# Compressed-branch logits with the keys stationary in four column groups, turned back for a four-head-wide softmax, in a one-core hybrid decoder block

## The chip, the cores and the metric

One core of one Trainium2 chip runs the program. The metric is the device time of one execution in microseconds; a kernel's time is the median over its runs. Every tensor is float32. The large products are made of three passes on split operands (a high part and the remainder, in a 32-bit format that TensorE reads in one pass).

## The reference, cut to what matters

The block is a token mixer of two branches (a gated delta rule and a native sparse attention) and a SwiGLU behind it, for 256 tokens and 1024 channels. The change sits in the compressed branch of the sparse attention: 8 heads in 2 groups, 15 compressed keys and values per group, two tiles of 128 tokens.

```python
kc = rmsnorm(compress(kc_raw, cmp_pe[0], cmp_w1[0], cmp_w2[0]), k_norm_w[0])   # (B, 15, G, 128)
vc = compress(vc_raw, cmp_pe[1], cmp_w1[1], cmp_w2[1])
lc = einsum("bqgrd,bngd->bgrqn", qb, kc) * scale + head_bias(t[:, None] - cmp_end[None, :])
pc = masked_softmax(lc, cmp_end[None, :] <= t[:, None])
oc = einsum("bgrqn,bngd->bqgrd", pc, vc)
o = gb[..., 0:1] * oc + gb[..., 1:2] * o_s + gb[..., 2:3] * ow
```

With 256 tokens the selected-block branch takes every block, so the other two branches are two causal attentions over 256 keys.

## The kernel before, in words

The program is written engine by engine, with semaphores by hand; nothing schedules it. All weights come as 87 chunks of 1 MB (`CHUNKS`), in order, through three buffers `raw`. For most chunks ACT makes `w_hi` (L502) and DVE `w_lo` (L791), two buffers of each, and PE runs 24 matmuls per half of a chunk (L1201 to L1203). The chunks of the compression MLP (`cmpk`, `cmpv`, four each) aren't split: PE runs four matmuls per half on four column groups, with 32 columns stationary and 256 moving (L1273).

Between the halves of the chunks, in slots (n, half), stand pieces of other work. Every engine walks through the same slots, and within a slot in the order: half chunk, stages of the delta rule, `misc`, attention `unit`.

- Stages of the delta rule (`gdn`): each goes over four groups of problems b = 0 to 3, in a ring of three PSUM banks, so that group 3 waits until the bank of group 0 has been read. In slots (24,0) to (27,1) they are X4, Y4, T4, X5, Y5, T5, X6, Z6; an X (L1367) or T (transposes of `Db`, L1206) is read by ACT (L643), a Y (L1333) by DVE (L929), Z6 is L1378. In (28,0), (28,1), (29,0) and (29,1) follow w0, s1, v1 and o1.
- `misc(m)`: the steps of the attention around one PSUM bank `log_ps`, each of which waits on PE for the output of the one before it (`m_out`). Before, in this order: W2_K and TURN_KC (compressed keys, turned into `kcT`), TURN_KS (24,1), TURN_KW (25,0), LOGITS_C (25,1), TURN_PC to TURN_PC+3 in (28,0), (28,1), (29,0), (29,1), and W2_V (30,0).
- LOGITS_C before: 16 matmuls on PE (L1433), one per head and token tile, with 128 columns of `nqT` stationary and 15 columns of `kcT` moving. Each is two records in the trace. DVE then masks, scales by the query norm, adds the bias and subtracts the maximum (L1028 to L1036), ACT takes the exponential (L681), DVE sums, divides and applies the gate (L1039 to L1045). On DVE all that stands in (25,1), ahead of the reading of Y5.
- TURN_PC before: 16 transposes in four slots of four (L1206), each read by ACT into `pcT` (L685) on 15 partitions.
- W2_V: four matmuls (L1423) and ACT's copy to `vc` (L678) on 15 partitions.
- Units: from (31,0) on, one per half chunk, over 8 heads by 2 token tiles. PE makes logits (L1449) once DVE has read those of the unit before (L1058, L1059), and adds the compressed branch's share by L1471.

In (29,1) ACT squares the delta rule's output (L662, 16 instructions), then does the rest of its slot, evacuates chunk 29 and makes `w_hi` of chunk 31; DVE makes `w_lo` of chunk 31 from that, and PE needs it for (31,0).

Of the kernel before, what the change touches and what calls it, by code (L numbers as in the profile page):

```python
# [119 lines left out]
def slot_solves(n, half):  # L120
# [5 lines left out]

W2_K, TURN_KC, TURN_KS, TURN_KW, LOGITS_C, TURN_PC, W2_V = 0, 1, 2, 3, 4, 5, 9
MISC_SLOTS = {W2_K: (AT["kw", 0], 0), TURN_KC: (AT["cmpv", 0], 0), TURN_KS: (AT["cmpv", 0], 1), TURN_KW: (AT["cmpv", 1], 0),
              LOGITS_C: (AT["cmpv", 1], 1),
              TURN_PC: (AT["vs", 0], 0), TURN_PC + 1: (AT["vs", 0], 1), TURN_PC + 2: (AT["vw", 0], 0), TURN_PC + 3: (AT["vw", 0], 1),  # L130
              W2_V: (AT["gz", 0], 0)}

# [11 lines left out]
def hybrid_block(nc, x, norm1_w, w_in, conv_w, a_log, dt_bias, gdn_norm_w, cmp_pe, cmp_w1, cmp_w2,  # L144
# [5 lines left out]
    with ctx:  # L150
# [329 lines left out]
        def _(act):  # L480
# [184 lines left out]
            def misc(m):  # L665
                if m in (TURN_KS, TURN_KW):
                    act.wait_ge(m_pe, m + 1)
                    j = 0 if m == TURN_KS else 1
                    dst = (ksT, kwT)[j][:].rearrange("p g (t c) -> p t g c", t=TT)
                    nc.scalar.activation(dst, log_ps[:].rearrange("p (t g c) -> p t g c", t=TT, g=GROUPS), ACT.Copy,  # L670
                                         scale=wk[:, 1 + j:2 + j]).then_inc(m_out, 1)
                elif m == TURN_KC:
                    act.wait_ge(m_pe, m + 1)
                    nc.scalar.activation(kcT[:, :, 0:NCMP], log_ps[:, 0:32].rearrange("p (g c) -> p g c", g=GROUPS)[:, :, 0:NCMP],
                                         ACT.Copy, scale=wk[:, 0:1]).then_inc(m_out, 1)
                elif m == W2_V:
# [99 lines left out]
        def _(dve):  # L776
# [238 lines left out]
            def misc(m):  # L1015
                if m == W2_K:
# [7 lines left out]
                    nc.vector.tensor_tensor(kc[:], kc[:], scol["d"][0:NCMP, 4:6].unsqueeze(2).to_broadcast([NCMP, GROUPS, DH]), ALU.mult).then_inc(m_out, 1)  # L1024
                elif m == LOGITS_C:
                    dve.wait_ge(m_pe, m + 1)
                    lg = log_ps[:, 0:HEADS * TT * 16].rearrange("p (h t n) -> p h t n", h=HEADS, t=TT)
                    link(nc.vector.memset(pc[:], NEG))  # L1028
                    for t in range(TT):
                        k = NCMP if t else (P - CMP_BLOCK) // CMP_STRIDE + 1  # L1030
                        first = P * (1 - t) + CMP_BLOCK - 1
# [10 lines left out]
                    link(nc.vector.tensor_scalar(pcs[:, :, 0], pcs[:, :, 0], rowvalid[:], None, ALU.mult))
                    g0 = gates[:].rearrange("p t (h b) -> p h t b", b=3)[:, :, :, 0]
                    link(nc.vector.tensor_tensor(pcs[:], pcs[:], g0, ALU.mult))
                    nc.vector.tensor_tensor(pc[:].rearrange("p h t n -> p (h t) n"), pc[:].rearrange("p h t n -> p (h t) n"),  # L1045
                                            pcs[:].rearrange("p h t -> p (h t)").unsqueeze(2).to_broadcast([P, 16, NCMP]), ALU.mult).then_inc(m_out, 1)

# [149 lines left out]
        def _(pe):  # L1197
# [209 lines left out]
            def misc(m):  # L1407

                if m >= 1:
                    pe.wait_ge(m_out, m)  # L1410
                if m in (TURN_KS, TURN_KW):
                    j = 0 if m == TURN_KS else 1
                    pe.wait_ge(key_n, j + 1)
                    for q in range(4):
                        last = transpose(log_ps[:, q * P:(q + 1) * P], key_tok[:, j, q, :])
                elif m in (W2_K, W2_V):
                    c = 0 if m == W2_K else 1
                    pe.wait_ge(hid_done, c + 1)
                    if c == 0:
                        pe.wait_ge(rk_ready, 1)  # L1420
                    for g in range(GROUPS):
                        for a in range(2):
                            last = pe.matmul(log_ps[0:NCMP, g * DH:(g + 1) * DH], hid[:, c, a, g * 16:g * 16 + NCMP], cmp2[:, c, a, :],  # L1423
                                             start=(a == 0), stop=(a == 1))
                elif m == TURN_KC:
                    for g in range(GROUPS):
                        last = transpose(log_ps[:, g * 16:g * 16 + NCMP], kc[:, g, :], NCMP)
                elif m == LOGITS_C:
                    pe.wait_ge(copied, COPY_NO[AT["nq", 3]] + 1)
                    for h in range(HEADS):  # L1430
                        for t in range(TT):
                            o = (h * TT + t) * 16
                            last = pe.matmul(log_ps[:, o:o + NCMP], nqT[:, h, t * P:(t + 1) * P], kcT[:, h // 4, 0:NCMP], start=True, stop=True)  # L1433
                else:
                    for q in range(4):
                        h, t = UNITS[4 * (m - TURN_PC) + q]
                        last = transpose(log_ps[0:NCMP, q * P:(q + 1) * P], pc[:, h, t, :])
                last.then_inc(m_pe, 1)

            def unit(i):  # L1440
                if i < len(UNITS):
                    h, t = UNITS[i]
                    w = P * (t + 1)
                    if i >= 1:
                        pe.wait_ge(s_done, i)
                    else:
                        pe.wait_ge(m_out, 10)
                    for a, keys in enumerate((ksT, kwT)):
# [114 lines left out]
```

## Time and profile before

| | |
|---|---|
| median of 3 runs | 647.7 us (646.86 to 649.11) |
| the profiled execution's own time | 654.54 us |
| its span, first to last instruction | 652.2 us |
| PE / DVE / ACT / POOL busy | 94% / 59% / 48% / 6% of the span |
| chain that ended last, by engine | PE 82%, DVE 10%, ACT 5%, issue 2%, DMA 1% |
| mean granted TensorE clock | 0.973 |
| DMA | 97.98 MB, 150 GB/s over the span |

"Idle before" in a row is the time its engine stood still ahead of it, with the one that ended it. "issue" names no other engine. PEclk in a table of windows is the TensorE clock that was granted, as a share of 2.4 GHz: 0.50 is 1.2 GHz. PE rows overlap, since matmuls are pipelined; the distance between the starts of two groups is what the first one takes.

### The profile page before, as it was taken

Reading aid. Unit: us, or ns where it says so; the run is one execution under the profiler, and the core shown is the slowest. Engines: PE = TensorE matmul, PEld = TensorE weight load, DVE = VectorE, ACT = ScalarE, POOL = GpSimd, SP = SyncE. Lnnn points to the kernel's source line nnn. Section 1 sums busy time; section 2 is a strip of 40 time slices with the busy share of each in tenths; the row PEclk is TensorE's granted clock in tenths of the full one; section 3 lists DMA queues with packets and bytes.
Section 4 is the critical chain, followed back from the end, with each engine's and each line's share of the span. In section 5 each row is a group of like instructions: output and inputs, shape, how many; then the busy total and the mean of one; then the engine's idle time right before and its main releaser. Section 6 shows DMA issues by size and latency. Waiting matters only on the chain.

```text
span 652.2 us, 10734 instructions
## 1 busy us (share of the span) xinstructions
PE 610.6 (94%) x4344; PEld 560.3 (86%) x4344; DVE 382.2 (59%) x651; ACT 311.7 (48%) x526; POOL 35.9 (6%) x55
## 2 busy tenths in 40 slices
PE   3998999998899999789899999997999999999996
PEld 2988999897798899789799999996888888888885
DVE  5566778773573534567746465555565566665553
ACT  5458864433325335554454454433655544444441
POOL 4100000330510000010000000000000000000000
PEclk9999999998989899989989999999799999999999
DMA  8942545165554262323333355547166666666631
GB/s 266 294 152 71 186 132 162 34 205 178 171 142 130 65 194 66 118 76 96 100 112 118 100 189 190 183 146 193 64 186 182 191 182 187 183 189 190 194 125 65
DMA packets 110458, 97.98 MB, mean 150 GB/s; under 512 B 4690, under 2 KB 106127, under 8 KB 110410
## 3 DMA queue, kind: packets, MB, share of 16 engines
q1 hardware_dynamic: 108272, 93.69, 47.2%
q0 software_dynamic: 1632, 2.47, 1.6%
q10 hardware_dynamic: 506, 1.14, 0.5%
q8 instruction: 35, 0.57, 0.4%
q14 instruction: 13, 0.11, 0.0%
HBM read 96.52 MB, written 1.45 MB: 150 GB/s over the span
## 4 chain that ended last, share of the span: by engine, by line
PE 82%; DVE 10%; ACT 5%; issue 2%; DMA 1%; DVEq 0%; ACTq 0%
PE ps L1201 15%; PE ps L1202 15%; PE ps L1203 15%; PE ps L1292 13%; PE ps L1295 6%; PE ps L1206 4%; PE ps L1333 4%; ACT w_hi L502 3%; DVE w_lo L791 3%; PE ps L1474 2%; PE ps L1367 2%; PE ps L1449 2%; PE ps L1273 1%; DVE cacc L884 1%; PE ps L1471 1%
## 5 line engine op out<-in xcount | busy, mean ns | idle before, releaser
L791 DVE TENSOR_TENSOR w_lo<-raw,w_hi 128x2048 fp32r<-128x2048 f32 x78 | 178.6, 2292 | 150.2 <-ACT w_hi L502 150.2
L502 ACT ACTIVATE w_hi<-raw 128x2048 fp32r<-128x2048 f32 x78 | 148.8, 1910 | 77.3 <-PE ps L1203 74.0
L1201 PE MATMUL ps<-h_both,w_hi 128*128 128x256 f32 x480 | 141.2, 294 | 5.4 <-ACT w_hi L502 3.0
L1202 PE MATMUL ps<-h_both,w_hi 128*128 128x256 f32 x480 | 137.9, 287 | 0.0
L1203 PE MATMUL ps<-h_both,w_lo 128*128 128x256 f32 x480 | 137.7, 287 | 0.0
L1292 PE MATMUL ps<-h_both,w_hi 128*128 128x512 f32 x352 | 122.9, 399 | 0.9 <-issue 0.9
L1201 PEld LDWEIGHTS ps<-h_both,w_hi 128*128 128x128 f32 x480 | 94.2, 196 | 7.6 <-issue 4.4
L1202 PEld LDWEIGHTS ps<-h_both,w_hi 128*128 128x128 f32 x480 | 94.3, 196 | 0.3 <-issue 0.2
L1203 PEld LDWEIGHTS ps<-h_both,w_lo 128*128 128x128 f32 x480 | 94.1, 196 | 0.0
L1295 PE MATMUL ps<-h_both,w_lo 128*128 128x256 f32 x352 | 91.5, 280 | 0.0
L1292 PEld LDWEIGHTS ps<-h_both,w_hi 128*128 128x128 f32 x352 | 64.2, 189 | 13.5 <-issue 1.1
L1295 PEld LDWEIGHTS ps<-h_both,w_lo 128*128 128x128 f32 x352 | 67.0, 190 | 3.8
L698 ACT ACTIVATE sc<-sc,s_nm 128x128 f32<-128x128 f32 (+1 forms) x32 | 14.3, 448 | 49.5 <-DVE s_nm L1059 49.5
L1201 PE MATMUL ps<-w_hi,g_hi 128*128 128x512 f32 x88 | 34.3, 389 | 0.0
L1202 PE MATMUL ps<-w_lo,g_hi 128*128 128x512 f32 x88 | 34.2, 389 | 0.0
L1203 PE MATMUL ps<-w_hi,g_lo 128*128 128x512 f32 x88 | 34.2, 389 | 0.0
L550 ACT ACTIVATE usum<-ps 128x256 f32<-128x256 f32 x22 | 8.4, 383 | 51.4 <-PE ps L1292 51.4
L884 DVE SCALAR_TENSOR_TENSOR cacc<-cin,cols_a,cacc 128x256 f32<-128x256 f32 x72 | 29.5, 478 | 0.0
L1201 PE MATMUL ps<-w_hi,h_both 128*128 128x256 f32 x64 | 19.8, 309 | 3.0 <-ACT w_hi L502 3.0
L1078 DVE TENSOR_TENSOR usum<-usum,ps 128x256 f32<-128x256 f32 x22 | 9.2, 420 | 18.3 <-ACT usum L550 18.3
L1202 PEld LDWEIGHTS ps<-w_lo,g_hi 128*128 128x128 f32 x88 | 16.5, 188 | 3.5
L1203 PEld LDWEIGHTS ps<-w_hi,g_lo 128*128 128x128 f32 x88 | 16.5, 188 | 3.5
(341 smaller groups left out, 1070.2 us busy)
## 6 DMA issues: line engine op xcount, KB each, us to landing
raw<-in_w_in SPq DMA_DIRECT2D x34, 1024.0 KB, 5.2
raw<-in_w_gate SPq DMA_DIRECT2D x22, 512.0 KB, 4.0
raw<-in_w_up SPq DMA_DIRECT2D x22, 512.0 KB, 5.3
raw<-in_w_down SPq DMA_DIRECT2D x11, 1024.0 KB, 4.9
raw<-in_cmp_w SPq DMA_DIRECT2D x8, 1024.0 KB, 6.1
raw<-in_w_proj_a SPq DMA_DIRECT2D x4, 1024.0 KB, 5.0
raw<-in_w_proj_b SPq DMA_DIRECT2D x4, 1024.0 KB, 5.1
raw<-in_w_out SPq DMA_DIRECT2D x4, 1024.0 KB, 5.1
```

What stands on the lines that cost most here:

```text
L502: nc.scalar.activation(w_hi[s % NSPL][:], raw[n % NRAW][:], ACT.Copy).then_inc(hi_done, 1)
L698: nc.scalar.activation(sc[i % 3][:, a, 0:w], sc[i % 3][:, a, 0:w], ACT.Exp, bias=scol["nm"][:, 2 * (i % 3) + a:2 * (i % 3) + a + 1], accum ...
L791: nc.vector.tensor_tensor(w_lo[s % NSPL][:], raw[n % NRAW][:], w_hi[s % NSPL][:].bitcast(f32), ALU.subtract).then_inc(lo_done, 1)
L884: ins = nc.vector.scalar_tensor_tensor(acc, src[:, a, j:j + SEQ], tap(k, a, j), acc, ALU.mult, ALU.add)
L1201: pe.matmul(bank, lhs(lh), rhs(rh), start=start, stop=False)
L1202: pe.matmul(bank, lhs(lh), rhs(rl), start=False, stop=False)
L1203: return pe.matmul(bank, lhs(ll), rhs(rh), start=False, stop=stop)
L1206: return pe.transpose(o, i, ident[0:n, 0:n])
L1292: cross = lambda stop: pe.matmul(bank[:], hi[:, k, half * P:(half + 1) * P], h_both[:, :, k, :], start=(k == 0), stop=stop)
L1295: last = pe.matmul(bank[:, 0:SEQ], lo[:, k, half * P:(half + 1) * P], h_hi[:, k, :], start=False, stop=False)
L1333: mm = lambda q, lhsT, rhs, start=True, stop=True: pe.matmul(b4[:, q, :], lhsT, rhs, start=start, stop=stop)
L1367: last = pe.matmul(b4[:, q, c], p4(ATb)[:, q, :], p4(Db)[:, q, c], start=True, stop=True)
```

## The change

- LOGITS_C moves to (25,0), ahead of TURN_KW. It is now four matmuls: 32 columns of `kcT` (15 keys, padded by zeros) stationary in column group c, the 512 columns of heads 2c and 2c+1 moving. The result has (column group, key) on the partitions. ACT copies it to `sc[0]` (512 columns).
- TURN_LC is new, in (26,0): four 128x128 transposes turn it back to tokens on the partitions, and DVE and ACT do the softmax, for each of the four blocks (head parity a, token tile t) four heads wide, with rows of 32 of which 15 count. On DVE it now stands behind the reading of Y5.
- TURN_PC is one step of four 128x128 transposes in (28,1), read by one ACT copy. (28,0), (29,0) and (29,1) have none.
- TURN_KW moves from (25,0) to (25,1). W2_V makes its product four times over, on four partition groups: eight matmuls with 16 columns stationary. In the units L1471 reads rows 32(h//2) and on.
- POOL clears `kcT` at the start.

```diff
+W2_K, TURN_KC, TURN_KS, LOGITS_C, TURN_KW, TURN_LC, TURN_PC, W2_V = range(8)
+MISC_SLOTS = {W2_K: (AT["kw", 0], 0), TURN_KC: (AT["cmpv", 0], 0), TURN_KS: (AT["cmpv", 0], 1), LOGITS_C: (AT["cmpv", 1], 0),
+              TURN_KW: (AT["cmpv", 1], 1), TURN_LC: (AT["cmpv", 2], 0), TURN_PC: (AT["vs", 0], 1), W2_V: (AT["gz", 0], 0)}
...
+            nc.gpsimd.memset(kcT[:], 0.0).then_inc(ones_set, 1)
...
                 elif m == LOGITS_C:
+                    act.wait_ge(m_pe, m + 1)
+                    nc.scalar.activation(sc[0][:].rearrange("p a c -> p (a c)"), log_ps[:], ACT.Copy).then_inc(m_out, 1)
+                elif m == TURN_LC:
                     act.wait_ge(pc_s, 1)
                     nc.scalar.activation(pc[:], pc[:], ACT.Exp).then_inc(pc_e, 1)
-                elif m >= TURN_PC:
+                elif m == TURN_PC:
                     act.wait_ge(m_pe, m + 1)
-                    q = 4 * (m - TURN_PC)
-                    nc.scalar.activation(pcT[:, q:q + 4, :], log_ps[0:NCMP, :].rearrange("p (a c) -> p a c", a=4), ACT.Copy).then_inc(m_out, 1)
+                    nc.scalar.activation(pcT[:], log_ps[:].rearrange("p (a c) -> p a c", a=2 * TT), ACT.Copy).then_inc(m_out, 1)
...
-                elif m == LOGITS_C:
+                elif m == TURN_LC:
                     dve.wait_ge(m_pe, m + 1)
...
                     link(nc.vector.memset(pc[:], NEG))
-                    for t in range(TT):
+                    for b in range(2 * TT):
+                        a, t = b // TT, b % TT
                         k = NCMP if t else (P - CMP_BLOCK) // CMP_STRIDE + 1
                         first = P * (1 - t) + CMP_BLOCK - 1
...
+                        link(nc.vector.tensor_tensor(pc[:, b, :, 0:k], lg[:, b, :, 0:k], of_head(col["rn"], a, t).unsqueeze(2).to_broadcast([P, 4, k]), ALU.mult))
+                        link(nc.vector.tensor_tensor(pc[:, b, :, 0:k], pc[:, b, :, 0:k],
+                                                     bias_g[:, a:HEADS:2, first:first + CMP_STRIDE * (k - 1) + 1:CMP_STRIDE], ALU.add))
+                    link(nc.vector.tensor_reduce(pcm[:], valid, AX.X, ALU.max))
+                    nc.vector.tensor_tensor(valid, valid, pcm[:].unsqueeze(3).to_broadcast([P, 2 * TT, 4, NCMP]), ALU.subtract).then_inc(pc_s, 1)
                     dve.wait_ge(pc_e, 1)
...
+                elif m == W2_V:
+                    pe.wait_ge(hid_done, 2)
+                    for a in range(2):
+                        for c in range(4):
+                            g = c // 2
+                            last = pe.matmul(log_ps[32 * c:32 * c + 16, 0:DH], hid[:, 1, a, g * 16:(g + 1) * 16], cmp2[:, 1, a, :],
                                              start=(a == 0), stop=(a == 1))
...
-                    for h in range(HEADS):
-                        for t in range(TT):
-                            o = (h * TT + t) * 16
-                            last = pe.matmul(log_ps[:, o:o + NCMP], nqT[:, h, t * P:(t + 1) * P], kcT[:, h // 4, 0:NCMP], start=True, stop=True)
...
+                    for c in range(4):
+                        last = pe.matmul(log_ps[32 * c:32 * c + 32, :], kcT[:, c // 2, :], nqT[:, 2 * c:2 * c + 2, :].rearrange("p h c -> p (h c)"),
+                                         start=True, stop=True)
+                elif m in (TURN_LC, TURN_PC):
+                    for b in range(2 * TT):
+                        src = sc[0][:].rearrange("p a c -> p (a c)")[:, b * P:(b + 1) * P] if m == TURN_LC else pc[:, b].rearrange("p c n -> p (c n)")
+                        last = transpose(log_ps[:, b * P:(b + 1) * P], src)
...
-                        pe.wait_ge(m_out, 10)
+                        pe.wait_ge(m_out, W2_V + 1)
...
+                    rows = slice(32 * (h // 2), 32 * (h // 2) + kk)
+                    pe.matmul(o, vc[rows, :], pcT[rows, (h % 2) * TT + t, :], start=True, stop=False)
```

The order of PE before, slots (25,0) to (27,0), from T4 (`ps<-ident,Db`) to X6 (`128x64`):

```order
L1206 MATMUL ps<-ident,Db 128x128 x16
L1206 MATMUL ps<-ident,key_tok 128x128 x4
L1273 MATMUL ps<-raw_50,flat 32x256 x4
L1367 MATMUL ps<-Db,ATb 128x128 x16
L1433 MATMUL ps<-kcT,nqT 128x15 x16
L1273 MATMUL ps<-raw_51,flat 32x256 x4
L1333 MATMUL ps<-AXb,DTb 128x128 x16
L1273 MATMUL ps<-raw_51,flat 32x256 x4
L1206 MATMUL ps<-ident,Db 128x128 x16
L1273 MATMUL ps<-raw_49,flat 32x256 x4
L1367 MATMUL ps<-Db,ATb 128x64 x16
```

The same stretch of PE in the changed kernel:

```order
L1212 MATMUL ps<-ident,Db 128x128 x16
L1442 MATMUL ps<-nqT,kcT 32x512 x4
L1279 MATMUL ps<-raw_50,flat 32x256 x4
L1373 MATMUL ps<-Db,ATb 128x128 x16
L1212 MATMUL ps<-ident,key_tok 128x128 x4
L1279 MATMUL ps<-raw_51,flat 32x256 x4
L1339 MATMUL ps<-AXb,DTb 128x128 x16
L1212 MATMUL ps<-ident,sc_122 128x128 x4
L1279 MATMUL ps<-raw_51,flat 32x256 x4
L1212 MATMUL ps<-ident,Db 128x128 x16
L1279 MATMUL ps<-raw_49,flat 32x256 x4
L1373 MATMUL ps<-Db,ATb 128x64 x16
```

The logits now stand right ahead of a half chunk, TURN_KW (`key_tok`) behind X5, and four transposes of `sc` (TURN_LC) between Y5 and T5.

On ACT, before, the reading of X5 (`AXb`), the exponential (`pc<-pc`) and the reading of T5 (`DTb`):

```order
L670 ACTIVATE kwT<-ps,wk 128x2x2x128
L643 ACTIVATE AXb<-ps 128x512 x4
L681 ACTIVATE pc<-pc 128x240
L643 ACTIVATE DTb<-ps 128x512 x4
L502 ACTIVATE w_hi_52<-raw_50 128x2048
```

And now:

```order
L681 ACTIVATE sc_122<-ps 128x512
L642 ACTIVATE AXb<-ps 128x512 x4
L669 ACTIVATE kwT<-ps,wk 128x2x2x128
L684 ACTIVATE pc<-pc 128x512
L642 ACTIVATE DTb<-ps 128x512 x4
L501 ACTIVATE w_hi_52<-raw_50 128x2048
```

The exponential keeps its place ahead of the reading of T5. On DVE the instructions that it waits for moved from ahead of the reading of Y5 to behind it:

```order
L992 TENSOR_TENSOR key_tok<-key_tok,s_c 128x512
L931 COPY_PREDICATED Db<-levels,ps 128x512 x8
L1032 MEMSET pc 128x512
L1037 TENSOR_TENSOR pc<-ps,c_rn 128x4x7
L1038 TENSOR_TENSOR pc<-pc,bias_g 128x4x7
```

Before, four of the eight (Y5's) stood behind the last instruction of the softmax.

## Rows read from the trace of the kernel before

**Rows 1.** Waits of PE, 264 to 375 us: total, times, longest

```profile
PE ps L1449 <- DVE s_nm L1059: 5.0, 3, 2.1
PE ps L1423 <- ACT pcT L685: 1.6, 1, 1.6
```

**Rows 2.** Timeline, PE, 205 to 224 us: start, us, instruction

```profile
205.82 0.60 PE L1206 MATMUL ps<-ident,key_tok 128*128 128x128 f32 x4
...
206.35 0.64 PE L1273 MATMUL ps<-raw,flat 128*32 128x256 f32 x8
...
206.92 3.84 PE L1367 MATMUL ps<-Db,ATb 128*128 128x128 f32 x32
...
210.60 3.64 PE L1433 MATMUL ps<-kcT,nqT 128*128 128x15 f32 x32
...
214.17 1.06 PE L1273 MATMUL ps<-raw,flat 128*32 128x256 f32 x8
...
215.16 4.12 PE L1333 MATMUL ps<-AXb,DTb 128*128 128x128 f32 x24
...
221.19 2.00 PE L1206 MATMUL ps<-ident,Db 128*128 128x128 f32 x16
...
223.69 3.79 PE L1367 MATMUL ps<-Db,ATb 128*128 128x64 f32 x32
```

**Rows 3.** Tile pc: duration ns min/median/max, first and last start us

```profile
L1032 DVE TENSOR_TENSOR pc<-ps,c_rn x2: 217/249/281, 214.7 to 215.2; 128x56 f32<-128x56 f32 x1, 128x120 f32<-128x120 f32 x1
L1033 DVE TENSOR_TENSOR pc<-pc,bias_g x2: 256/307/358, 214.9 to 215.5; 128x56 f32<-128x56 f32 x1, 128x120 f32<-128x120 f32 x1
L1028 DVE MEMSET pc<- x1: 258/258/258, 214.4 to 214.4; 128x240 f32 x1
L1035 DVE TENSOR_REDUCE pcm<-pc x1: 402/402/402, 215.9 to 215.9; 128x16 f32<-128x240 f32 x1
L1036 DVE TENSOR_TENSOR pc<-pc,pcm x1: 408/408/408, 216.3 to 216.3; 128x240 f32<-128x240 f32 x1
L681 ACT ACTIVATE pc<-pc x1: 403/403/403, 216.8 to 216.8; 128x240 f32<-128x240 f32 x1
```

**Rows 4.** Timeline: Y4 on PE, its last reading on DVE, T4's on ACT

```profile
199.22 3.84 PE L1333 MATMUL ps<-AXb,DTb 128*128 128x128 f32 x32
...
203.09 0.73 DVE L929 COPY_PREDICATED Db<-levels,ps 128x512 f32<-128x512 uint8 x1 [0.16 <-PE ps L1333]
...
204.68 2.07 ACT L643 ACTIVATE DTb<-ps 128x512 f32<-128x512 f32 x4 [0.47 <-PE ps L1206]
```

**Rows 5.** Windows: us, busy of PE, PEld, DVE, ACT, POOL; PEclk, DMA share, GB/s

```profile
262.70:264.30 1.60, 0.01 (x1) 0.02 (x2) 0.00 (x0) 1.60 (x10) 0.00 (x0) 1.00 0.00 0
264.30:268.40 4.10, 4.09 (x32) 3.60 (x32) 1.78 (x1) 2.47 (x3) 0.00 (x0) 1.00 0.00 0
284.00:285.90 1.90, 0.08 (x2) 0.04 (x1) 1.84 (x4) 0.06 (x1) 0.00 (x0) 1.00 0.00 0
285.90:289.40 3.50, 3.50 (x10) 2.47 (x10) 2.21 (x6) 1.09 (x5) 0.00 (x0) 0.51 0.88 293
320.50:322.60 2.10, 0.00 (x0) 0.00 (x0) 2.07 (x6) 0.00 (x0) 0.00 (x0) 1.00 1.00 283
322.60:330.30 7.70, 7.66 (x32) 6.55 (x33) 3.69 (x11) 5.33 (x14) 0.00 (x0) 0.56 0.17 58
...
214.26:217.60 3.34, 3.34 (x19) 2.53 (x20) 2.56 (x8) 0.40 (x1) 0.00 (x0) 0.50 0.00 0
```

**Rows 6.** The chain that ended last: the first of the four TURN_PC

```profile
238.70 0.44 PE ps L1206 x4
```

**Rows 7.** Timeline, 266 to 277 us, DVE and PE

```profile
266.62 2.29 DVE L791 TENSOR_TENSOR w_lo<-raw,w_hi 128x2048 fp32r<-128x2048 f32 x1 [5.30 <-ACT w_hi L502]
269.01 0.36 PE L1201 MATMUL ps<-h_both,w_hi 128*128 128x256 f32 x1 [0.62 <-issue]
276.51 0.70 PE L1449 MATMUL ps<-ksT,nqT 128*128 128x256 f32 x2 [1.07 <-DVE s_nm L1059]
```

More of the change, by code:

```diff
@@ L121, in slot_solves @@
     return 2 * (n - FIRST_STAGE_SLOT) + half - 1 == BEFORE_SOLVE + SOLVE_AFTER
[L127 to L131, printed above, removed]
+W2_K, TURN_KC, TURN_KS, LOGITS_C, TURN_KW, TURN_LC, TURN_PC, W2_V = range(8)
+MISC_SLOTS = {W2_K: (AT["kw", 0], 0), TURN_KC: (AT["cmpv", 0], 0), TURN_KS: (AT["cmpv", 0], 1), LOGITS_C: (AT["cmpv", 1], 0),
+              TURN_KW: (AT["cmpv", 1], 1), TURN_LC: (AT["cmpv", 2], 0), TURN_PC: (AT["vs", 0], 1), W2_V: (AT["gz", 0], 0)}
 def slot_misc(n, half):
@@ L180, in hybrid_block @@
         key_tok = at("key_tok", yb_at + 12 * KB, [P, 2, 4, DH])
-        pcT = at("pcT", yb_at, [NCMP, 16, P])
+        pcT = at("pcT", yb_at + 9 * KB, [P, 2 * TT, P])
+        pcm = at("pcm", yb_at + 11 * KB, [P, 2 * TT, 4])
+        pcs = at("pcs", yb_at + 11 * KB + 64, [P, 2 * TT, 4])
         arena = take(72 * KB)
@@ L265, in hybrid_block @@
         xs = own("xs", [P, TT, 4])
-        kcT = own("kcT", [P, GROUPS, 16])
+        kcT = own("kcT", [P, GROUPS, 32])
         ps = [ctx.enter_context(nc.psum_tensor(f"ps{i}", [P, 512], f32)) for i in range(8)]
@@ L1024, in misc @@
                     nc.vector.tensor_tensor(kc[:], kc[:], scol["d"][0:NCMP, 4:6].unsqueeze(2).to_broadcast([NCMP, GROUPS, DH]), ALU.mult).then_inc(m_out, 1)
-                elif m == LOGITS_C:
+                elif m == TURN_LC:
                     dve.wait_ge(m_pe, m + 1)
-                    lg = log_ps[:, 0:HEADS * TT * 16].rearrange("p (h t n) -> p h t n", h=HEADS, t=TT)
+                    lg = log_ps[:].rearrange("p (b c n) -> p b c n", b=2 * TT, c=4)
+                    of_head = lambda hts, a, t: hts[:, :, t].rearrange("p (c a) -> p a c", a=2)[:, a, :]
+                    valid = pc[:, :, :, 0:NCMP]
@@ L1038, in misc @@
+                        link(nc.vector.tensor_tensor(pc[:, b, :, 0:k], pc[:, b, :, 0:k],
+                                                     bias_g[:, a:HEADS:2, first:first + CMP_STRIDE * (k - 1) + 1:CMP_STRIDE], ALU.add))
+                    link(nc.vector.tensor_reduce(pcm[:], valid, AX.X, ALU.max))
+                    nc.vector.tensor_tensor(valid, valid, pcm[:].unsqueeze(3).to_broadcast([P, 2 * TT, 4, NCMP]), ALU.subtract).then_inc(pc_s, 1)
                     dve.wait_ge(pc_e, 1)
-                    link(nc.vector.tensor_reduce(pcs[:].rearrange("p h t -> p (h t)"), pc[:].rearrange("p h t n -> p (h t) n"), AX.X, ALU.add))
+                    link(nc.vector.tensor_reduce(pcs[:], valid, AX.X, ALU.add))
@@ L1040, in misc @@
                     link(nc.vector.reciprocal(pcs[:], pcs[:]))
[L1042 to L1046, printed above, removed]
+                    by_t = pcs[:].rearrange("p (a t) c -> p t a c", t=TT)
@@ new lines, in misc @@
+                    link(nc.vector.tensor_scalar(by_t[:, 0], by_t[:, 0], rowvalid[:], None, ALU.mult))
+                    g0 = gates[:].rearrange("p t (c a b) -> p t a c b", a=2, b=3)
+                    for t in range(TT):
+                        ins = nc.vector.tensor_tensor(by_t[:, t], by_t[:, t], g0[:, t, :, :, 0], ALU.mult)
+                    link(ins)
+                    nc.vector.tensor_tensor(valid, valid, pcs[:].unsqueeze(3).to_broadcast([P, 2 * TT, 4, NCMP]), ALU.mult).then_inc(m_out, 1)
@@ L1415, in misc @@
                         last = transpose(log_ps[:, q * P:(q + 1) * P], key_tok[:, j, q, :])
[L1416 to L1420, printed above, removed]
+                elif m == W2_K:
+                    pe.wait_ge(hid_done, 1)
+                    pe.wait_ge(rk_ready, 1)
                     for g in range(GROUPS):
                         for a in range(2):
-                            last = pe.matmul(log_ps[0:NCMP, g * DH:(g + 1) * DH], hid[:, c, a, g * 16:g * 16 + NCMP], cmp2[:, c, a, :],
+                            last = pe.matmul(log_ps[0:NCMP, g * DH:(g + 1) * DH], hid[:, 0, a, g * 16:g * 16 + NCMP], cmp2[:, 0, a, :],
+                                             start=(a == 0), stop=(a == 1))
+                elif m == W2_V:
[4 more added lines that the diff above has]
+                            last = pe.matmul(log_ps[32 * c:32 * c + 16, 0:DH], hid[:, 1, a, g * 16:(g + 1) * 16], cmp2[:, 1, a, :],
                                              start=(a == 0), stop=(a == 1))
@@ L1429, in misc @@
                     pe.wait_ge(copied, COPY_NO[AT["nq", 3]] + 1)
-                    for h in range(HEADS):
-                        for t in range(TT):
-                            o = (h * TT + t) * 16
-                            last = pe.matmul(log_ps[:, o:o + NCMP], nqT[:, h, t * P:(t + 1) * P], kcT[:, h // 4, 0:NCMP], start=True, stop=True)
[L1434 to L1437, printed above, removed]
+                    for c in range(4):
[5 more added lines that the diff above has]
+                        last = transpose(log_ps[:, b * P:(b + 1) * P], src)
                 last.then_inc(m_pe, 1)
@@ L1470, in unit @@
                     kk = NCMP if t else (P - CMP_BLOCK) // CMP_STRIDE + 1
-                    pe.matmul(o, vc[0:kk, g, :], pcT[0:kk, j, :], start=True, stop=False)
+                    rows = slice(32 * (h // 2), 32 * (h // 2) + kk)
+                    pe.matmul(o, vc[rows, :], pcT[rows, (h % 2) * TT + t, :], start=True, stop=False)
                     for a, values in enumerate((vs, vw)):
```

15 lines of the change are left out of this document (4 added, 11 removed).

## The prediction

> **What bounds the kernel now.** The chain that ended last is PE for 82% of the span, so I read PE's waits first and the timeline of the slots that change next. Between 205 and 262 us PE hardly waits for another engine. Behind that, up to 375 us, stand two waits that matter here: 1.6 us for ACT's last `pcT` copy, and three waits of units for DVE, 5.0 us in all [rows 1]. So until 262 us what PE issues is the time, and the logits alone, 16 matmuls of 15 moving columns, take from 210.60 to 214.17: 3.57 us [rows 2]. A second cost stands right behind them. From 214.26 to 217.6 PE is granted 1.2 GHz instead of 2.4 [rows 5], though it was never idle before: what it ran was the 15-column matmuls. The half chunk at 214.17 takes 0.99 us instead of 0.57 (206.35 to 206.92), and three quarters of Y5 behind it 4.12 us [rows 2], where all of Y4 takes 3.84 us [rows 4].
>
> All sums go by the profiled execution (span 652.2 us, own time 654.54 us, 1.1% above the median 647.7 us). I apply the differences to the median unscaled. About 0.3% (2 us) is what a measurement of this kernel can tell from no change.
>
> **Term A, slots (25,0) to X6.** I count from 205.82, where T4 ends in both. Before, X6 starts at 223.69: 17.87 us [rows 2]. The changed order on PE, if it never waits:
> - four logits matmuls with 512 columns. The four of a half chunk, also on four column groups but with 256 columns, take 0.57 us up to the next work, of which I put 0.15 down to the change of work. Twice the columns: 2 x 0.42 + 0.15 = 1.0. Bounds: 0.57 below; above 3.6, if the groups don't overlap (Y4's 32 records of 128 columns start 0.112 apart [rows 4], so eight of 512 would take 8 x 0.45; for 256 columns the same sum gives 1.8, and the row shows 0.57). I take 1.0, since the nearest row overlaps.
> - half chunk 0.57, X5 3.68 (206.92 to 210.60), TURN_KW 0.53, half chunk 0.57, Y5 3.68 at full clock: so Y5 starts at 205.82 + 1.0 + 0.57 + 3.68 + 0.53 + 0.57 = 212.17.
> - TURN_LC 0.53 (as TURN_KW), half chunk 0.57, T5 and a half chunk 2.50 (221.19 to 223.69).
> Together 1.0 + 0.57 + 3.68 + 0.53 + 0.57 + 3.68 + 0.53 + 0.57 + 2.50 = 13.63: X6 at 219.45, 4.24 us earlier.
>
> But there is a new wait. ACT now reaches the reading of T5 only behind the exponential, and the exponential waits for DVE, which starts on the logits only behind Y5. DVE ends its last copy of Y4 at 203.82, 4.60 us after Y4's start [rows 4]; the same behind Y5 gives 216.77. Then, from the durations of [rows 3] with 0.04 us between linked instructions (2.18 us of work lie between 214.4 and 216.8):
> - memset of 512 instead of 240 columns: 0.258 + 272 x 1.05 ns = 0.54;
> - two pairs on 28 elements and two on 60, read off the line through 56 and 120: multiply 0.19 and 0.22, add 0.21 and 0.26, so 2 x 0.40 + 2 x 0.48 = 1.76;
> - maximum 0.40, subtraction 0.41; ten gaps 0.4.
> That is 3.51 us: 220.28. The exponential of 512 columns takes 0.6 (0.40 for 240, and ACT's copies of 512 take some 0.6), the reading of T5's first group another 0.6 [rows 4]: 221.45. PE has made three groups of T5 by 216.95 + 3 x 0.45 = 218.30 and then stands still, since the ring has three banks, for **3.15 us**. X6 starts at 222.6, 1.1 us earlier than before instead of 4.24. If the new DVE instructions cost nothing beyond their old 2.4 us the wait is 2.1; if each strided one costs 0.1 more it is 4.
>
> A rule speaks against the change here. The Trainium skill, TensorEngine Tiling (Array Packing), section Performance Considerations, says that tiling speeds up TensorE but not the evacuation of PSUM, so that the copy may become the bottleneck. By PE's own rows alone the term would be 4.24 us; by that rule it's the 1.1.
>
> **The clock behind that wait.** The trace has stretches in which PE was idle and what followed: after 1.9 us at 284 it was granted 1.2 GHz for 3.4 us, after 2.1 us at 320.5 for most of 7.7 us (0.56 on average), after 1.6 us at 262.7 it kept 2.4 GHz [rows 5]. A wait of 3.15 us is longer than all of these, so I expect a stretch at 1.2 GHz. Part of it falls into the wait, and X6 has only 64 columns per pass, so that the weights set its pace: I take 1.3 us, between 0.4 (most of it hidden) and 3.4 (a long one as at 322.6). The old stretch behind the 15-column logits is in the 17.87 us, so it's already counted as gone. Term A: 1.1 - 1.3 = **-0.2 us**.
>
> **Term B, TURN_PC.** Four steps become one. Two of the removed ones, in (28,0) and (29,0), stand ahead of o1 on a PE that doesn't wait: 2 x 0.44 [rows 6] = **0.9 us**. The one kept has 128 instead of 15 partitions, and the transposes have the same 128 columns: nothing. ACT's copy is of 512 columns as before.
>
> **Term C, from o1 to unit 1.** The third removed step was the one PE waited for 1.6 us [rows 1]. That wait goes, but not into the time: chunk 31 can't start before its `w_lo`, which ends at 268.91, and PE starts at 269.01 [rows 7]. `w_lo` hangs on `w_hi`, and this on ACT's queue behind the 16 squares; what leaves this queue is one `pcT` copy, 0.5 us. So PE's two waits, 1.6 and 0.6, become one of about 2.4 ahead of chunk 31. W2_V's eight matmuls instead of four lie ahead of it and cost nothing; were the wait gone, they'd cost at most their eight further records, 0.9 us. Behind chunk 31, `gate_t` and `w_hi` of chunk 32 come up to 1.8 us earlier, since PE ends (30,1) sooner, and with them DVE reaches unit 0 sooner; the 1.07 us that unit 1 waits [rows 7] go. At full clock: 0.5 + 1.07 = 1.6 us. But a wait of 2.4 us lies above the 1.9 and 2.1 that were followed by 1.2 GHz; with that, most of it is given back. I take **+0.6 us**.
>
> **Nothing:** the units' L1471 keeps its 32-row tile and its columns, whichever partition group it reads; ACT's copy of the logits to `sc` (0.6 us) is hidden behind X5; TURN_KW's copy behind the half chunk and Y5; POOL's memset of 64 columns (0.1 us) is ahead of small DMAs whose data PE needs much later. If X5 didn't hide ACT's copy, TURN_KW would wait 0.6.
>
> Sum: -0.2 + 0.9 + 0.6 = 1.3 us, so 647.7 - 1.3 = **646.4 us**.
>
> **The rivals.**
> 1. *The clock holds through both waits* (or the waits are short). Then A is 1.1, C is 1.6: 3.6 us less, 644.1. For it: the clock held after 1.6 us. Against: it fell after both longer ones. 0.25.
> 2. *Slower: the new wait before the last quarter of T5 sets off a long stretch of 1.2 GHz, as at 322.6.* T5, X6 and Z6 are transposes and narrow matmuls, much like what ran there. It decides when PE runs at 1.2 GHz for over 4 us after the wait. Such a stretch costs 3.4 us instead of 1.3, and a second like it after chunk 31's wait turns C from +0.6 to -1.9: 1.1 - 3.4 + 0.9 - 1.9 = -3.3, so 651.0. With the first alone: 1.1 - 3.4 + 0.9 + 0.6 = -0.8, 648.5. 0.13 in all.
> 3. *The four column groups don't overlap with 512 columns.* The logits cost 3.6 instead of 1.0, and DVE's chain starts 2.6 later: 1.3 - 2.6 = -1.3, 649.0. Against it is the half chunk. 0.07.
>
> **How the numbers follow.** My forecast has 0.55: both waits, both followed by a slow stretch of ordinary length. Its own spread is 645.0 to 647.8. Faster by over 0.3%: rival 1 nearly whole (0.24) and a fifth of the forecast (0.12): 0.36. Slower by over 0.3%: half of rival 2, some of rival 3, and stretches of 1.2 GHz that fall elsewhere in the later waits (one costs 1.7 us): 0.13. Within: 0.51. The range leaves out the ends of rivals 1 and 2: 643.0 to 649.8.
>
> **What would show it.** The four logits matmuls in about 1.0 us, and 2.4 GHz in the half chunk and Y5 behind them. PE idle for some 3 us before the last four transposes of T5, with ACT's reading of T5 behind the exponential. No idle time before W2_V, some 2.4 us before chunk 31, none before unit 1. Two new windows at 0.5 behind these waits. I'm wrong if T5 goes through without a wait, if the clock holds behind 3 us of idle time, or if L1471 takes longer from the other partition groups.

## The result, and the profile after

The change makes the kernel slower: 654.73 us median of 6 runs (654.04 to 656.0) against 649.88 (646.86 to 652.75) for the kernel before, ratio 1.008 with a 95% interval of 1.0046 to 1.0113. The profiled execution has a span of 653.7 us. The medians here and below are of all runs, while a ratio leaves out runs of a slower state: one of the kernel before at 2630 us, and four of the ten of e1, at 651.0 to 651.4 us, which stand over 1.5% above that kernel's fastest, 641.23.

Its order on PE is the predicted one, and so is nearly every duration up to the new wait. The timeline of PE and ACT, from T4 on (start, us, engine, instruction), answers to [rows 2]. The times of a trace count from its own first instruction, and T4 begins anywhere from 202.1 to 204.2 us, ahead of the slots that the change touches. So I compare two traces by the distance from T4's start (203.99 in the kernel before, 204.22 here).

```profile
204.22 2.00 PE L1212 MATMUL ps<-ident,Db 128*128 128x128 f32 x16
...
206.15 1.06 PE L1442 MATMUL ps<-nqT,kcT 128*32 128x512 f32 x8
...
207.03 0.61 PE L1279 MATMUL ps<-raw,flat 128*32 128x256 f32 x8
...
207.58 3.84 PE L1373 MATMUL ps<-Db,ATb 128*128 128x128 f32 x32
...
212.35 3.84 PE L1339 MATMUL ps<-AXb,DTb 128*128 128x128 f32 x32
...
217.13 1.53 PE L1212 MATMUL ps<-ident,Db 128*128 128x128 f32 x12
...
220.43 0.63 ACT L684 ACTIVATE pc<-pc 128x512 f32<-128x512 f32 x1 [7.80 <-DVE pc L1041]
...
221.59 1.12 PE L1212 MATMUL ps<-ident,Db 128*128 128x128 f32 x4 [2.94 <-ACT DTb L642]
...
223.65 7.09 PE L1373 MATMUL ps<-Db,ATb 128*128 128x64 f32 x32
...
231.68 7.09 PE L1384 MATMUL ps<-DTb,AXb 128*128 128x64 f32 x32
238.53 0.56 PE L1207 MATMUL ps<-w_hi,h_both 128*128 128x256 f32 x1
```

The logits take 0.88 us up to the half chunk instead of 3.57, and the half chunk and Y5 behind them run at full speed. Then PE stands still for 2.9 us, and what comes next is the surprise: X6 and the half chunk behind it take 8.0 us (223.65 to 231.68) and Z6 6.9, 14.88 together, where before all that was through in 7.87 us. Chunk 28 starts at 238.53, 34.31 us behind T4's start, before at 231.56, 27.57 us behind it. The table of windows (busy of PE, PEld, DVE, ACT, POOL; then PEclk, DMA share, GB/s), for the wait and for what follows:

```profile
218.47:221.59 3.12, 0.18 (x2) 0.00 (x0) 2.18 (x9) 1.16 (x3) 0.00 (x0) 0.98 0.97 310
221.20:241.40 20.20, 19.81 (x97) 17.74 (x98) 7.64 (x12) 7.31 (x11) 0.00 (x0) 0.51 0.36 114
```

For 20 us PE runs at 1.2 GHz, though it is busy for 19.8 of them. In the whole trace of the kernel before, no stretch at that clock was longer than about 7 us.

The waits of PE further on, from 235 to 300 us (total, times, longest), answer to [rows 1]:

```profile
PE ps L1207 <- ACT w_hi L501: 2.7, 1, 2.7
PE ps L1459 <- DVE s_nm L1065: 1.8, 1, 1.8
```

The wait of W2_V is gone, one of 2.7 us stands ahead of chunk 31 instead (with 1.2 GHz behind it from 276 to 279.5), and unit 1 waits no more. Unit 1's logits start 79.67 us behind T4's start (283.89), before 72.52 (276.51): up to here the change costs 7.2 us.

In the two profiled executions the spans differ by only 1.5 us, since the one of the kernel before fell to 1.2 GHz behind two later waits (at 285.9 and 322.6, [rows 5]), and the changed one, with waits of the same length (1.8 and 2.1 us) that end at 293.1 and 328.6, didn't:

```profile
292.90:300.00 7.10, 6.72 (x47) 5.72 (x47) 3.93 (x13) 5.17 (x13) 0.00 (x0) 1.00 0.47 149
...
329.00:336.00 7.00, 6.86 (x51) 5.88 (x50) 3.21 (x9) 4.93 (x13) 0.00 (x0) 1.00 0.13 44
```

So these two profiles show where the time goes, but their totals don't measure it; the medians do.

### The profile page after: what moved, and what is told of

The parts are those of the page before. It is cut to its first block, busy times and chain, and to the rows that moved or that the text cites. A ratio compares the mean times of both kernels' runs of the same rounds, so it can differ in the third digit from the quotient of the medians.

```text
span 653.7 us, 10691 instructions
## 1 busy us (share of the span) xinstructions
PE 610.1 (93%) x4320; PEld 559.9 (86%) x4320; DVE 383.1 (59%) x656; ACT 311.1 (48%) x524; POOL 36.0 (6%) x56
## 4 chain that ended last, share of the span: by engine, by line
PE 82%; DVE 9%; ACT 5%; issue 2%; DMA 1%; DVEq 0%; ACTq 0%
PE ps L1207 15%; PE ps L1208 15%; PE ps L1209 15%; PE ps L1298 13%; PE ps L1301 6%; PE ps L1339 4%; PE ps L1212 4%; ACT w_hi L501 3%; DVE w_lo L793 2%; PE ps L1373 2%; PE ps L1485 2%; PE ps L1279 1%; PE ps L1459 1%; PE ps L1384 1%; DVE cacc L886 1%
## 5 line engine op out<-in xcount | busy, mean ns | idle before, releaser
L1207 PE MATMUL ps<-w_hi,h_both 128*128 128x256 f32 x64 | 20.6, 321 | 3.0 <-ACT w_hi L501 3.0
L1208 PE MATMUL ps<-w_lo,h_both 128*128 128x256 f32 x64 | 19.8, 310 | 0.0
L1209 PE MATMUL ps<-w_hi,h_both 128*128 128x256 f32 x64 | 19.8, 309 | 0.0
```

The costliest lines, as they stand in the source:

```text
L1207: pe.matmul(bank, lhs(lh), rhs(rh), start=start, stop=False)
L1208: pe.matmul(bank, lhs(lh), rhs(rl), start=False, stop=False)
L1209: return pe.matmul(bank, lhs(ll), rhs(rh), start=False, stop=stop)
```

## The experiments

The open question was what keeps TensorE at 1.2 GHz for 20 us: the wait, the new layout, or the work behind the wait. Four kernels take these apart. The matmuls that e2, e4, e6 and e8 add write a free PSUM bank that nobody reads. I call them wide: they have 512 moving columns, in the format that TensorE reads in one pass, so each is one record of the trace where an fp32 matmul of X6 is two.

**e1: the exponential behind the reading of T5.** Only ACT's order changes.

```diff
                     for m in slot_misc(n, half):
-                        misc(m)
+                        if m != TURN_LC:
+                            misc(m)
+                    if (n, half) == (AT["cmpv", 2], 1):
+                        misc(TURN_LC)
```

> The changed kernel with ACT's exponential behind the reading of T5 instead of ahead of it. Theory (the wait starts it): the change is slower because PE waits 2.9 us ahead of the last quarter of T5, falls to 1.2 GHz there and stays there for 20 us. Then this kernel has no wait in T5, no stretch at 1.2 GHz between 218 and 241, X6 and Z6 take 3.7 us each instead of 8.0, and chunk 28 starts at about 227.5 instead of 238.5. The time falls by 3 us of wait and about 9 of slow work, partly taken back by the later waits: 643 to 649 us, below the kernel before or equal. Rival (the new layout itself is slow, or the narrow matmuls bring the clock down anyway): the wait goes, the slow stretch stays, 651 to 653 us.

Measured: 650.46 us against 650.6 for the kernel before, ratio 0.995 (0.9906 to 0.9995). PE's timeline:

```profile
216.49 2.00 PE L1215 MATMUL ps<-ident,Db 128*128 128x128 f32 x16
218.42 0.64 PE L1282 MATMUL ps<-raw,flat 128*32 128x256 f32 x8
218.99 2.89 PE L1376 MATMUL ps<-Db,ATb 128*128 128x64 f32 x24
222.53 1.10 PE L1376 MATMUL ps<-Db,ATb 128*128 128x64 f32 x8 [0.65 <-ACT AXb L642]
223.57 0.64 PE L1282 MATMUL ps<-raw,flat 128*32 128x256 f32 x8
224.14 3.79 PE L1387 MATMUL ps<-DTb,AXb 128*128 128x64 f32 x32
227.73 0.36 PE L1210 MATMUL ps<-w_hi,h_both 128*128 128x256 f32 x1
```

T5 goes through, the clock is 1.00 in the window from 216 to 241, and chunk 28 starts 24.14 us behind T4's start (227.73, T4 at 203.59): 3.4 us earlier than in the kernel before and 10.2 earlier than with the change. Only a wait of 0.65 us ahead of the last quarter of X6 is new.

The time, 650.46 us, lies above the 643 to 649 that were expected. Later stretches took part of the gain back: 1.2 GHz for 3.4 us behind the 2.7 us ahead of chunk 31, and for 6.8 us each from 282 and from 319.6, behind waits of units that in the changed kernel's profile kept 2.4 GHz. One run took 641.23 us; its mean granted clock was 0.982, that of the other nine 0.968 to 0.970. One move on ACT takes the change from slower to level with the kernel before by the medians. The ratio, which counts six of the ten runs, puts it slightly below; that is not shown.

**e2: wide work in place of the wait.**

```diff
+                    if name == "T5" and b == 3:
+                        for _ in range(14):
+                            pe.matmul(ps[7][:], h_hi[:, 0, 0:P], h_both[:, 0, 0:2, :].rearrange("p k c -> p (k c)"), start=True, stop=True)
```

> The changed kernel with 14 matmuls of 512 columns, whose result nobody reads, on PE ahead of the last quarter of T5, where it waits: about 3 us of wide work in place of the wait. The wait for ACT stays where it ends. Theory (idle time brings the clock down): 2.4 GHz up to chunk 28, X6 starts at 222.6 to 223.2 and takes 3.7 us, chunk 28 starts at 230 to 231; 645 to 650 us. Rival (the clock falls by what runs around the wait, transposes and narrow matmuls, or by the layout): a slow stretch all the same, 654 to 656 us.

Measured: 647.31 us, ratio 0.9933 (0.9904 to 0.9961). In PE's timeline the 14 matmuls fill the wait; the last quarter of T5 starts 4.59 us behind T5's start (219.65, T5 at 215.06), in the changed kernel 4.46 (221.59, 217.13), so they overshoot it by 0.1 us:

```profile
216.34 3.46 PE L1335 MATMUL ps<-h_both 128*128 128x512 f32 x14
219.65 0.60 PE L1212 MATMUL ps<-ident,Db 128*128 128x128 f32 x4
...
220.74 3.79 PE L1376 MATMUL ps<-Db,ATb 128*128 128x64 f32 x32
225.03 3.79 PE L1387 MATMUL ps<-DTb,AXb 128*128 128x64 f32 x32
```

and the windows over them and the 20 us behind:

```profile
216.30:219.70 3.40, 3.40 (x18) 2.75 (x17) 2.46 (x9) 1.35 (x3) 0.00 (x0) 1.00 0.97 303
219.70:240.00 20.30, 20.30 (x183) 19.24 (x182) 7.58 (x12) 9.59 (x19) 0.00 (x0) 1.00 0.49 156
```

ACT's exponential starts 3.29 us behind T5's start (218.35), in the changed kernel 3.30 (220.43); only the idle time is gone, and the clock holds through T5, X6 and Z6. The layout isn't at fault. Chunk 28 starts 26.47 us behind T4's start (228.62, T4 at 202.15), 7.8 us earlier than in the changed kernel, as expected. Useless work makes that kernel 7 us faster by the medians, 654.73 and 647.31, each from its own group of runs, with the kernel before at 649.88 and at 650.6.

**e3: the wait in the kernel before.**

```diff
+                    if name == "T5" and b == 0:
+                        act.wait_ge(g_mm, u + 1)
+                        for _ in range(5):
+                            link(nc.scalar.activation(sc[0][:], sc[0][:], ACT.Copy))
```

> The kernel before, with five copies of 512 columns on ACT ahead of the reading of T5, so that PE waits some 3 us ahead of the last quarter of T5; nothing else of the change. Theory (the wait and the narrow work behind it are enough): PE falls to 1.2 GHz in the wait and stays there through X6 and Z6 into chunk 28; 3 us of wait and about 9 of slow work, 658 to 664 us. Rival (a wait of 3 us costs itself and an ordinary stretch of 3.4 us at 1.2 GHz): 652 to 655 us. Rival (it is the new layout): 652 to 653 us, with no long stretch.

Measured: 664.3 us, ratio 1.0163 (1.0078 to 1.0248); three runs lie at 664.0 to 664.8, one at 655.31. Timeline and windows:

```profile
224.19 1.11 PE L1210 MATMUL ps<-ident,Db 128*128 128x128 f32 x4 [3.12 <-ACT DTb L647]
225.24 1.08 PE L1277 MATMUL ps<-raw,flat 128*32 128x256 f32 x8
226.25 7.09 PE L1371 MATMUL ps<-Db,ATb 128*128 128x64 f32 x32
233.27 1.08 PE L1277 MATMUL ps<-raw,flat 128*32 128x256 f32 x8
234.28 7.09 PE L1382 MATMUL ps<-DTb,AXb 128*128 128x64 f32 x32
```

```profile
223.90:244.40 20.50, 20.21 (x100) 18.14 (x101) 6.24 (x6) 7.22 (x11) 0.00 (x0) 0.51 0.34 106
```

With none of the change but a wait of 3.1 us in the same place, the same 20.5 us at 1.2 GHz come: the wait suffices. Chunk 28 starts 38.80 us behind T4's start (241.13, T4 at 202.33), 11.2 us later than in the kernel before. The three longer runs lie at and just above the upper end of the 658 to 664 us expected. The run at 655.31 has no profile, but its mean granted clock was 0.975, theirs 0.960 to 0.963. By my estimate from these clocks it spent some 16 us less at 1.2 GHz, so the long stretch was most likely missing there: the fall doesn't follow every time.

**e4: wide work behind the wait.** As e2, but 16 matmuls ahead of X6; the wait stays.

> The changed kernel with 16 matmuls of 512 columns, whose result nobody reads, ahead of X6, that is behind the wait: 3.5 us of wide work at 2.4 GHz, 6.9 at 1.2. Theory (narrow work behind the wait keeps the clock down): the clock is back at 2.4 GHz some 4 to 7 us behind the wait, X6 and Z6 take 3.7 us each, chunk 28 starts about 2 to 4 us earlier than at 238.5 in spite of the added work; 650 to 654 us. Rival (the stretch of 20 us has its own length, whatever runs): X6 and Z6 take 8 us as before, and the added work is paid in full, 660 us and more.

Measured: 654.15 us, ratio 1.0065 (1.0043 to 1.0086).

```profile
223.45 6.00 PE L1335 MATMUL ps<-h_both 128*128 128x512 f32 x16
229.28 3.68 PE L1376 MATMUL ps<-Db,ATb 128*128 128x64 f32 x32
233.46 3.79 PE L1387 MATMUL ps<-DTb,AXb 128*128 128x64 f32 x32
```

```profile
221.00:227.80 6.80, 6.41 (x22) 4.42 (x23) 3.73 (x7) 3.71 (x5) 0.00 (x0) 0.51 0.09 29
227.80:241.00 13.20, 13.20 (x112) 12.39 (x111) 3.96 (x5) 3.60 (x6) 0.00 (x0) 1.00 0.50 156
```

The clock falls in the wait as before but is back 6.8 us later, during the wide matmuls, and then holds through the same X6 and Z6 that otherwise ran at 1.2 GHz from end to end. Chunk 28 starts 33.03 us behind T4's start (237.06, T4 at 204.03), 1.3 us earlier in spite of 5.8 us of added work; 2 to 4 were expected, and the time is 0.15 us above its range. So X6 and Z6 didn't bring the clock down and don't do so at 2.4 GHz, in e2 or here; but with them behind the wait it doesn't come back either, until the 256-column matmuls of chunk 28. A stretch with a length of its own, whatever runs, is out. Not separated is what about the wide matmuls counts: they differ from those of X6 and Z6 in their columns and in their format, and no run has fp32 matmuls of 512 columns there.

**e5 and e9: both new waits taken away.** e1, and ACT's evacuation of chunk 29 and `w_hi` of chunk 31 ahead of the squares.

```diff
-                    if not conv_phase:
+                    if not conv_phase and n != AT["gz", 0]:
                         evacuate(n - 1)
...
-                    if n + 1 < len(CHUNKS):
+                    if n + 1 < len(CHUNKS) and n != AT["gz", 0]:
                         split_hi(n + 1)
...
+                    if (n, half) == (AT["vw", 0], 1):
+                        evacuate(n)
+                        split_hi(n + 2)
                     for name in slot_stages(n, half):
                         gdn(name)
```

> The changed kernel with the exponential behind the reading of T5, and with ACT's evacuation of chunk 29 and w_hi of chunk 31 ahead of the 16 squares of (29,1) instead of behind them. Theory: both waits that the change made are gone (2.9 us ahead of T5's last quarter, 2.7 us ahead of chunk 31), and with them the stretches at 1.2 GHz behind them. Against the kernel before it saves the logits' 2.6 us, the 1.7 us that it lost to 1.2 GHz behind them, 1.3 us of TURN_PC and 3.3 us of waits at 262 to 276: 641 to 646 us, ratio 0.985 to 0.993. Rival (the waits for DVE in the units grow by what is won): 647 to 650 us.

> The kernel of e5 again, on the same chip as e8, so that the two are compared with the same runs of the kernel before: 643 to 646 us.

Measured: 644.39 us, ratio 0.9901 (0.9865 to 0.9937), and again, on the chip of e8, 643.01, ratio 0.9886 (0.9856 to 0.9917). PE's waits from 200 to 345 us in e5:

```profile
PE ps L1465 <- DVE s_nm L1071: 5.9, 3, 2.2
PE ps L1379 <- ACT AXb L642: 0.7, 1, 0.7
```

Both waits are gone. The rival is right in part: unit 1 waits for DVE again, 1.9 us. Both times lie in the range expected or at its lower end.

**e7: the second move alone, in the kernel before.**

> The kernel before with only the second of these moves: evacuation of chunk 29 and w_hi of chunk 31 ahead of the squares. Theory: its waits of 1.6 us (W2_V) stays, since W2_V waits for the last pcT copy behind the squares, while the 0.6 us before chunk 31 and the 1.1 us before unit 1 go: 1 to 2 us less, ratio 0.997 to 0.999, and the rest of e5's gain is the changed kernel's own. Rival (the gain of e5 is all in this move): ratio 0.99 or less.

Measured: 651.95 us, ratio 1.0018 (0.9993 to 1.0043): no gain, where 0.997 to 0.999 was expected. Its waits from 255 to 300 us:

```profile
PE ps L1452 <- DVE s_nm L1062: 2.8, 2, 1.9
PE ps L1426 <- ACT pcT L685: 2.5, 1, 2.5
```

What was put ahead of the squares delays the last `pcT` copy behind them, so W2_V waits 2.5 instead of 1.6 us, and PE falls to 1.2 GHz there (264 to 268). The wait ahead of chunk 31 is gone as expected, but that of unit 1 grows from 1.1 to 1.9 us. So the gain of e5 isn't in this move by itself; it goes with the last `pcT` copy having left that slot.

**e6: wide matmuls between the old logits.** The kernel before, with one matmul of 512 columns behind each of the 16.

> The kernel before with one matmul of 512 columns, whose result nobody reads, behind each of the 16 logits matmuls. Theory (the 15-column matmuls, on a PE that is never idle, brought the clock down at 214): with wide work between them the clock stays at 2.4 GHz, the half chunk behind takes 0.57 us instead of 0.99 and three quarters of Y5 2.7 us instead of 4.1; the logits take 3.6 + 16 x 0.22 = 7.1 us. Rival (something else brought it down): 1.2 GHz again behind them.

One run, 653.57 us, too few to compare times:

```profile
216.32 0.64 PE L1273 MATMUL ps<-raw,flat 128*32 128x256 f32 x8
216.89 2.94 PE L1333 MATMUL ps<-AXb,DTb 128*128 128x128 f32 x24
```

The clock is 1.00 in the window from 205 to 230; the half chunk takes 0.57 us instead of 0.99, three quarters of Y5 2.94 instead of 4.12. The three traces with the old logits alone (before, e3, e7) all have 3.4 us at 1.2 GHz behind them, and none with the new ones has. So the fall belonged to the 15-column matmuls standing there without other work. The added matmuls take 3.7 us of their own, though (208.97 to 216.32 for the logits with them), and after the quick three quarters Y5 waits 1.5 us for DVE.

**e8: wide work in the waits of units 1 and 3.** e5 with nine matmuls of 512 columns ahead of each.

> The kernel of e5 with nine matmuls of 512 columns, whose result nobody reads, on PE ahead of the logits of unit 1 and of unit 3, where e5 waits 1.9 and 1.8 us for DVE. The waits end when they ended before, so no work is saved. Theory (a wait of PE costs itself and, where the clock falls behind it, about half of the slow stretch): the 6.8 us at 1.2 GHz behind unit 3's wait go, about 3 us where PE is the bound: 640 to 643 us, ratio 0.983 to 0.989. Rival (the units are bound by DVE there, so that PE's clock costs nothing): 644 to 645 us, as e5. Rival (the filler overshoots the waits): 645 us and more.

Measured: 641.23 us, ratio 0.9871 (0.9825 to 0.9917). PE's timeline at units 3 and 4 and the window behind unit 3's logits, in e9 and then in e8:

```profile
277.12 0.98 PE L1465 MATMUL ps<-ksT,nqT 128*128 128x256 f32 x2 [1.82 <-DVE s_nm L1071]
...
285.56 0.39 PE L1465 MATMUL ps<-ksT,nqT 128*128 128x128 f32 x2
...
277.20:285.00 7.80, 7.80 (x34) 6.76 (x35) 3.96 (x11) 5.06 (x13) 0.00 (x0) 0.56 0.39 135
```

```profile
277.16 2.23 PE L1462 MATMUL ps<-h_both 128*128 128x512 f32 x9
...
279.22 0.62 PE L1468 MATMUL ps<-ksT,nqT 128*128 128x256 f32 x2
...
284.80 0.39 PE L1468 MATMUL ps<-ksT,nqT 128*128 128x128 f32 x2
...
277.20:285.00 7.80, 7.66 (x50) 6.47 (x50) 5.54 (x14) 4.32 (x13) 0.00 (x0) 1.00 0.42 135
```

T4 starts 2.0 us later in e8's trace than in e9's, so the two windows don't hold the same work; the distance between the logits of units 3 and 4 does, and it is 5.58 us instead of 8.44. The profiled spans, counted from T4's start, also differ by 3.0 us. The median falls by 1.8 us against e9 on the same chip, but the two intervals overlap widely, and one of the six runs was at 647.51. That the slow stretch goes and 2.9 us with it is shown for these two executions; that the median falls is likely only.

## Why the prediction was wrong

The forecast was 646.4 us, the result 654.73. Of the difference, 2.2 us are the kernel before itself, whose median is 649.88 over six runs where the prediction had 647.7 from three. Up to unit 1 the two profiles can be set against the sum, terms A, B and C, forecast as -0.2, 0.9 and 0.6 us gained: they measure -8.2, 0.9 and 0.2. So term A holds nearly all of the miss.

- **The logits and the old slow stretch: right.** 1.0 us forecast, 0.88 measured. The four column groups overlap at 512 columns too, so rival 3 is out, and e6 supports the reason given for the old stretch.
- **The new wait: right.** The prediction had the last copy of Y5 end at 216.77, ACT's exponential start at 220.28 and PE wait until 221.45, 3.15 us; it was 216.97, 220.43 and 221.59, 2.9 us of idle time. X6 was to start at 222.6 at full clock; the clock fell about 0.1 us before the wait ended, so the last quarter of T5 ran at 1.2 GHz, and X6 started at 223.65. The rule of the Trainium skill that was quoted (TensorEngine Tiling (Array Packing), Performance Considerations: tiling speeds up TensorE but not the evacuation of PSUM) points the right way: 2.7 us are won on the logits, and the path through DVE and ACT behind them holds PE for 2.9. But e1, where the wait is gone with the same copies and the same softmax, shows that its cause was the exponential's place in ACT's queue, not the rate of evacuation.
- **The clock behind that wait: the step that failed.** "Part of it falls into the wait, and X6 has only 64 columns per pass, so that the weights set its pace: I take 1.3 us, between 0.4 (most of it hidden) and 3.4 (a long one as at 322.6)." Only 0.1 us of the stretch fell into the wait, and it lasted 20 us, not 3.4 to 7. The pace of the weight loads isn't spared by the clock either: the 32 loads of X6 took 6.90 us where they took 3.65 before, and X6 and Z6 took twice as long (7.09 against 3.79 us). From X6 to chunk 28 it is 14.88 us instead of 7.87, so 7.0 for these two, 1.0 around the end of T5 and 1.5 in the first half of chunk 28 (4.46 us for 24 matmuls instead of 2.95; the clock was back at 241.9): 9.5 us where 1.3 stood, against a bound of 3.4.
- **The nearest rows were left out.** The prediction compared its wait with three of 1.6 to 2.1 us. The kernel before also has two of 3.04 us, each ahead of a chunk of 256-column matmuls:

```profile
159.60 0.52 PE L1201 MATMUL ps<-h_both,w_hi 128*128 128x256 f32 x1 [3.04 <-ACT w_hi L502]
...
178.67 0.55 PE L1201 MATMUL ps<-w_hi,h_both 128*128 128x256 f32 x1 [3.04 <-ACT w_hi L502]
```

```profile
159.60:163.50 3.90, 3.90 (x20) 3.90 (x21) 3.61 (x10) 0.00 (x0) 0.00 (x0) 0.56 0.91 284
178.70:183.50 4.80, 4.80 (x22) 4.80 (x23) 4.35 (x15) 0.00 (x0) 2.42 (x5) 0.50 1.03 281
```

Both were followed by 1.2 GHz, which ended within 5 us of chunk work; in the second the clock had fallen already 2 us before the wait ended. They would have made the fall near certain, but not told its length ahead of T5, X6 and Z6: I read the length of a slow stretch off others of the same trace and didn't ask what work would be there to end this one.

- **Rival 2 named the mechanism and the place,** a wait ahead of the last quarter of T5 and then X6 and Z6 at 1.2 GHz, at 0.13 and 648.5 to 651.0 us. Its size came from the window of 7.7 us at 322.6 [rows 5], a good third of the real stretch, and its 3.4 us a third of the real cost. The range ended at 649.8 for the same reason.
- **TURN_PC (term B): right.** From the end of chunk 28's first half to o1, with the granted clock at 1.00 in both, PE takes 22.02 us (242.99 to 265.01) instead of 22.90 (234.51 to 257.41): 0.88 us for two steps, 0.9 forecast.
- **From o1 to unit 1 (term C): right in its waits, 0.2 us instead of 0.6.** From o1's start to unit 1's logits it is 18.88 us, before 19.10. No idle time ahead of W2_V, 2.7 us ahead of chunk 31 (2.4 forecast), none ahead of unit 1, and 1.2 GHz behind the new wait. Chunk 31 to unit 1's logits takes 7.74 us (276.15 to 283.89) against 7.50 before (269.01 to 276.51).
- **L1482 from other partition groups costs nothing,** as expected: its records take 270 to 372 ns, before 270 to 577, when one unit ran at the low clock.

## What to carry to other kernels

When a step on TensorE becomes faster by moving its results through two more engines, work out when those engines give back what TensorE needs next; if it waits, move what nobody waits for (here the exponential) behind what it waits for. And price a wait of TensorE not by its length alone but by the work that stands behind it: in this kernel the stretch at 1.2 GHz lasted 6.8 us with wide matmuls behind the wait (e4) and 20 us with transposes and fp32 matmuls of 64 columns, where 2.9 us of waiting cost 9.5 us more. e5, the change with two moves on ACT's queue, is 1% faster than the kernel before; a median of two or three runs isn't enough to see such differences here, as the kernel before itself runs from 647 to 655 us, apart from one run at 2630.

## What the runs showed that was not expected

- TensorE can stay at 1.2 GHz for 20 us while it is busy for 98% of the time by the profile (19.81 of 20.20 us), and the same matmuls hold 2.4 GHz when it was at 2.4 GHz before them (e2, e4).
- Whether the clock falls behind a wait of 2 to 3 us isn't settled by its length. The 2.7 us ahead of chunk 31 were followed by 1.2 GHz in the changed kernel and e1, but in e2 and e4 the granted clock was 1.00 for the 4 us behind the same wait; the units' waits of 1.8 and 2.1 us went either way too. All five waits of 2.9 to 3.1 us that I looked at (two before, one each in the changed kernel, e3 and e4) were followed by 1.2 GHz. What decides it stays open.
- fp32 matmuls of 64 columns, whose start-to-start pace of 0.11 us is no better than that of 128 columns (32 records take 3.79 and 3.84 us), fall to 0.22 at 1.2 GHz.
- W2_V's eight matmuls on four column groups took less than the four in one group: 0.63 us against 1.05.

```profile
269.76 0.63 PE L1434 MATMUL ps<-cmp,hid 128*16 128x128 f32 x16
```

- Filling a wait of TensorE with useless wide matmuls can pay for itself: 7 us by the medians in e2, against the same kernel without them.
